# Modulation sums shared with GpSimd and a forget gate by quarters of the array, in a one-layer encoder kernel

## The chip, the cores and the metric

The kernel runs on one core of one Trainium2 chip. The metric is the device time of one execution in microseconds; the time before is the median of three executions. The core's engines are TensorE (PE in the profile), VectorE (DVE), ScalarE (ACT), GpSimd (POOL, called Pool here) and SyncE (SP), which only issues transfers here.

## What is computed

The reference is one layer of a hybrid encoder on 512 tokens of width 1024, all in f32. What matters here is its beginning:

```python
c_act = jax.nn.silu(c)
mod = c_act @ ada_w + ada_b                     # (1024) @ (1024, 6144)
sh1, sc1, g1, sh2, sc2, g2 = jnp.split(mod, 6, axis=-1)
h = modulate(rms_norm(x, mix_norm_g), sh1, sc1) # h * (1 + scale) + shift
z = h @ w_in                                    # q, k, v of mixers A and B, f_raw, ga, gb
log_f = jax.nn.log_sigmoid(f_raw + b_fgate)     # 8 heads: the forget gate
```

Behind it come two attention mixers (8 heads of 64 each), their merge, the output projection, and a mixture of 64 experts (top 8) with a shared expert. The change touches only the product c_act @ ada_w for sh1 and sc1, and the eight columns f_raw of h @ w_in.

## The kernel before, in words

**Modulation sums.** The 6144 columns of ada_w are taken in 24 steps of 256 columns, u = 0 to 23. A step's tile has 8 blocks k of 128 rows: [128, 8, 256]. ada_sum(u) on VectorE (lines 861 to 876) multiplies block 0 by the column cact[:, 0] (L871) and adds seven blocks, each times its own column of cact (L873), into one of four accumulators ACC (u mod 4). TensorE then sums over the 128 partitions with a matmul against ones. Steps 0 to 7 are sh1 and sc1, in pairs p = 0 to 3: ada_by_feature(u) (line 1300) brings the sum of step u into two PSUM columns, and mod_columns(p) on VectorE (line 895) makes of both steps the shift and scale columns for two blocks of h. Steps 8 to 23 are spread over all partitions, four at a time (spread_group, line 1350) and added to MOD. Their tiles go through two buffers AD; the tiles of the first eight steps have places of their own (AF, line 190).

**The head.** SyncE issues, in this order: the small rows, tiles 0 and 1, x in four parts, two blocks of w_in, tiles 2 and 3, two blocks of w_in, tiles 4 and 5, and so on to tile 7. VectorE does ada_sum(0) and ada_sum(1), then x_row(t) for the four token tiles (x times its reciprocal root; the roots come from ScalarE, L679 and L680) mixed with take_xt_first(t), the copy of half of the turned x out of PSUM; then three times two sums and mod_columns (lines 903 to 917). TensorE turns the rows, does ada_by_feature(0) and (1) between rows 1 and 2, and then project_first (line 1327): the first 512 columns of w_in with the contraction outermost, since block k of h can be used as soon as ScalarE has applied its shift and scale (modulate, line 690). Behind step k of it stands ada_by_feature(k + 2).

**The rest of the projection.** project(i, b) (line 1340) makes 512 further columns of z with h stationary, 32 matmuls of 128x128 by 512, on a block of w_in that SyncE loads into one of two places. Each f32 matmul has two records in the trace. forget (line 1318) makes the eight forget columns as 32 matmuls, h stationary [128x128], with 8 moving columns of WF. TensorE's order is written out: project_first, project(0, 1), forget, spread_group(0), project(1, 0), spread_group(1), project(1, 1), spread_group(2), the cumulative sum of log_f (L1368), project(2, 0) and so on (lines 1355 to 1376). VectorE's log_forget (line 919) follows sums 8 to 11; behind it come sums 12 to 23 and the additions mod_add (L879).

**SyncE's queue.** load_ada(u) (line 439) for u from 8 waits until sum u - 2 is done, since that frees its buffer. After load_ada(8) and load_ada(9) come load_w(1), the block for project(0, 1) (L446), then four rows of ada_b, the gain and the bias table (lines 466 to 476). Pool has nothing to do before the bias table lands (L559).

Of the kernel before, what the change touches and what calls it, by code (L numbers as in the profile page):

```python
# [25 lines left out]
P = 128  # L26
# [3 lines left out]
HA = 8  # L30
NH = 16
NT = S // P
KD = D // P
# [11 lines left out]
HC = 256  # L45
# [73 lines left out]
C_N = 1086 + NMAIN  # L119


def constants():

    c = np.zeros((P, C_N), np.float32)
    p = np.arange(P)[:, None]
    f = np.arange(P)[None, :]
    c[:, C_ID:C_ID + P] = p == f
    c[:, C_TEX:C_TEX + P] = p < f
    c[:, C_TIN:C_TIN + P] = p <= f
    c[:, C_ONE:C_ONE + P] = 1.0  # L130
    c[:, C_SLOT:C_SLOT + P] = f + 1
    token = p + P * np.arange(NT)[None]
    c[:, C_TOK2 + T_HI:C_TOK2 + 8:2] = token // 8 * 8 - NOTOK
    c[:, C_TOK2 + T_LO:C_TOK2 + 8:2] = token % 8
    c[:, C_M:C_M + NEXT] = np.arange(NEXT)[None]
    c[:, C_E:C_E + 1] = p
    c[:, C_LOW:C_LOW + 64] = (np.arange(8)[None, :] < np.arange(8)[:, None]).reshape(1, 64)
    c[:, C_SC:C_SC + 3] = [EPS, DH * EPS, 1.0]
    c[:, C_NEG1:C_NEG1 + P] = -1.0
    column = np.arange(E)  # L140
    c[:, C_CJ:C_CJ + NMAIN] = np.concatenate([column, SECOND])[None]
    cap = np.where(column < NFULL, P, P // 2)
    cap[SECOND[0]] = 2 * P
    cap[list(SECOND[1:])] = P + P // 2
    cap[NWIDE:NFULL] = NARROW
    c[:, C_CAP:C_CAP + E] = cap[None]
    c[:, C_LT:C_LT + E] = column[None] < p
    c[:, C_BR:C_BR + 2] = [3000.0, 2000.0]
    c[0:2, C_BC] = [3000.0, 2000.0]
    causal = np.zeros((P, S), np.float32)  # L150
    causal[:, S - P:] = np.where(f > p, NEG, 0.0)
    return c, causal


def build(nc, a):
# [4 lines left out]
    with st:  # L160
# [63 lines left out]
        def tab(at):  # L224
# [29 lines left out]
        WF = sb("WF", [P, KD, HA])  # L254
# [72 lines left out]
            "down_done", "o_ready", "row_index_ready"))  # L327
        s_out = sem("residual_written")
# [101 lines left out]
        def _(sp):  # L430
# [8 lines left out]
            def load_ada(u):  # L439
                sp.wait_ge(s_acc, u - 1)  # L440
                sp.dma_start(AD[:, u % 2], ada_step(u)).then_inc(s_ada[u % 2], 16)
# [24 lines left out]
            sp.dma_start(WF[:, :, :], w_in[:, 6 * SEG:6 * SEG + HA].rearrange(  # L466
# [18 lines left out]
            sp.wait_ge(s_acc, 24)  # L485
# [70 lines left out]
        def _(pool):  # L556
            pool.memset(CUM[:, :, :, 0:HA], 0.0).then_inc(s_pch, 1)
            pool.wait_ge(s_tab, 16)
# [3 lines left out]
            pool.wait_ge(s_acc, 24)  # L562
# [295 lines left out]
        def _(dve):  # L858
# [45 lines left out]
            ada_sum(1)  # L904
# [9 lines left out]
            for p in range(1, 4):  # L914
                ada_sum(2 * p)
                ada_sum(2 * p + 1)
                mod_columns(p)

            def log_forget():

                dve.wait_ge(s_f, 1)
                dve.wait_ge(s_small, 32)
                link(dve.tensor_tensor(FZ[:, 0], PS[:, 6, 0:32].rearrange("p (t h) -> p t h", t=NT),
# [350 lines left out]
        def _(pe):  # L1274
# [25 lines left out]
            def ada_by_feature(u):  # L1300

                p, r = u // 2, u % 2
                pe.wait_ge(s_acc, u + 1)
# [14 lines left out]
            def forget():  # L1318

                pe.wait_ge(s_wf, 16)  # L1320
                for t in range(NT):
                    for k in range(KD):
                        ins = mm(PS[:, 6, HA * t:HA * t + HA], HT[:, k, P * t:P * t + P], WF[:, k, :],
                                 start=k == 0, stop=k == KD - 1)
                ins.then_inc(s_f, 1)
# [24 lines left out]
            def spread_group(g):  # L1350
                pe.wait_ge(s_acc, 12 + 4 * g)
                need(pe, s_madd, 4 * g)
                spread(range(8 + 4 * g, 12 + 4 * g))
# [4 lines left out]
            spread_group(0)  # L1358
            project(1, 0)
# [5 lines left out]
            pe.wait_ge(s_cst, 16)  # L1365
# [358 lines left out]
```

## Time and profile before

| what | value |
|---|---|
| median of 3 executions | 1313.33 us (1310.59 to 1315.42) |
| the profiled execution, its own time | 1317.05 us |
| its span | 1315.1 us |
| mean granted TensorE clock | 0.964 |
| TensorE busy | 1211.5 us (92%), 4649 matmul records |
| VectorE, ScalarE, Pool busy | 480.9, 197.8, 192.7 us |

The profile is of one execution. Its times count from the start of the span. TensorE's matmuls overlap each other, so its busy time is not its useful time: what counts is when an instruction starts against the one before, and what ended the engine's idle time. The chain of waits, followed back from the last instruction, says which engine set the end at each moment.

### The profile page before, as it was taken

The numbers are of one execution on the slowest core, as the hardware profiler recorded it, in microseconds if no ns is written. First come the engines' busy times: TensorE is split into PE (matmuls) and PEld (weight loads), VectorE is DVE, ScalarE is ACT, GpSimd is POOL, SyncE is SP. The second block draws the span as 40 slices with busy tenths as digits, with TensorE's granted clock in tenths as the row PEclk, the third lists the DMA queues.
The fourth block names the chain that finished last, engine by engine and source line by source line (L and its number), as shares of the span: only waits on it lengthen the run. The fifth ranks groups of instructions, "written<-read, shape, count | busy, mean of one in ns | idle before, by whom it ended". The sixth has DMA issues, their size and how long they took to land.

```text
span 1315.1 us, 13938 instructions
## 1 busy us (share of the span) xinstructions
PE 1211.5 (92%) x4649; PEld 618.2 (47%) x4649; DVE 480.9 (37%) x1280; ACT 197.8 (15%) x451; POOL 192.7 (15%) x219
## 2 busy tenths in 40 slices
PE   4899999999999999998899999797999898999985
PEld 3455454444788644444444444343444343444442
DVE  5725457400466322455233233132233222333322
ACT  3211001110566101120011011010011001011100
POOL 0000000000221000000022222122222221313212
PEclk9998999999999999998899899899999899999988
DMA  9775562211100302165479999999989999989972
GB/s 323 248 268 192 192 220 107 81 64 64 65 0 0 128 1 104 64 256 240 189 281 361 395 359 360 374 358 374 373 287 378 388 367 388 381 268 376 360 207 34
DMA packets 87327, 311.51 MB, mean 237 GB/s; under 512 B 12225, under 2 KB 37985, under 8 KB 62049
## 3 DMA queue, kind: packets, MB, share of 16 engines
q1 hardware_dynamic: 71040, 272.77, 53.6%
q0 software_dynamic: 14784, 35.68, 11.6%
q10 hardware_dynamic: 1440, 2.27, 0.5%
q8 instruction: 35, 0.57, 0.2%
q14 instruction: 28, 0.22, 0.0%
HBM read 295.46 MB, written 34.08 MB: 251 GB/s over the span
## 4 chain that ended last, share of the span: by engine, by line
PE 74%; DMA 18%; DVE 3%; issue 2%; SPq 1%; ACT 1%; POOL 0%; DVEq 0%; POOLq 0%; ACTq 0%
PE PS L1634 19%; PE PS L1346 19%; PE PS L1655 9%; DMA R_WT<-w_up_e 9%; PE PS L1513 4%; PE PS L1484 4%; PE PS L1620 3%; PE PS L1417 2%; PE PS L1393 2%; DMA out<-second_sum 2%; DMA R_Z<-w_up_e 2%; DMA R_XM<-w_up_e 2%; PE PS L1523 2%; PE PS L1291 1%; PE PS L1405 1%
## 5 line engine op out<-in xcount | busy, mean ns | idle before, releaser
L1346 PE MATMUL PS<-R_WT,R_HT 128*128 128x512 f32 x576 | 248.9, 594 | 1.3 <-DMA R_WT<-w_in 1.3
L1634 PE MATMUL PS<-R_Z,R_G 128*128 128x512 f32 (+1 forms) x496 | 202.8, 627 | 12.8 <-DMA R_Z<-w_up_e 10.8
L1346 PEld LDWEIGHTS PS<-R_WT,R_HT 128*128 128x128 f32 x576 | 109.7, 191 | 138.2 <-issue 135.8
L1634 PE MATMUL PS<-R_WT,R_G 128*64 128x512 f32 (+1 forms) x400 | 144.2, 621 | 22.9 <-DMA R_Z<-w_up_e 18.0
L1209 DVE TENSOR_TENSOR R_G<-R_G,PS 128x256 f32<-128x256 f32 x50 | 30.5, 610 | 367.7 <-ACT R_G L821 367.7
L1634 PEld LDWEIGHTS PS<-R_Z,R_G 128*128 128x128 f32 (+1 forms) x496 | 75.6, 172 | 109.0 <-issue 109.0
L615 POOL DMA_INDIRECT R_G<-h_rows,gidx x54 | 56.1, 1040 | 447.7 <-DVE gidx L1198 371.5
L826 ACT ACTIVATE R_G<-PS 128x256 f32<-128x256 f32 x50 | 19.2, 385 | 572.8 <-PE PS L1642 556.8
L1655 PE MATMUL PS<-R_Z,R_G 128*128 128x512 f32 (+1 forms) x248 | 101.3, 610 | 0.8 <-issue 0.8
L1634 PEld LDWEIGHTS PS<-R_WT,R_G 128*64 128x64 f32 (+1 forms) x400 | 52.3, 160 | 100.7 <-issue 100.7
L1230 DVE SCALAR_TENSOR_TENSOR R_G<-PS,slx,R_XM 128x512 f32<-128x512 f32 x100 | 75.0, 751 | 63.5 <-PE PS L1655 63.5
L1634 PE MATMUL PS<-R_XM,R_G 128*128 128x512 f32 (+1 forms) x208 | 93.2, 601 | 4.4 <-DMA R_WT<-w_up_e 4.4
L621 POOL DMA_INDIRECT out<-R_G,ridx x38 | 55.9, 1470 | 106.9 <-DVE R_G L1230 48.8
L1655 PE MATMUL PS<-R_WT,R_G 128*64 128x512 f32 (+1 forms) x200 | 69.6, 599 | 0.0
L1620 PE MATMUL PS<-cst,R_G 128*128 128x128 f32 x416 | 56.7, 281 | 13.4 <-DMA R_G<-h_rows,gidx 12.5
L985 DVE CUSTOM_DVE_ANT_0 R_S<-PS,R_A 128x128 f32<-128x128 f32 (+1 forms) x64 | 28.9, 489 | 106.9 <-PE PS L1393 106.4
L873 DVE SCALAR_TENSOR_TENSOR R_A<-R_WT,cact,R_A 128x256 f32<-128x256 f32 x126 | 61.1, 485 | 4.5
L1620 PEld LDWEIGHTS PS<-cst,R_G 128*128 128x128 f32 x416 | 49.1, 146 | 14.8 <-DMA R_G<-h_rows,gidx 13.6
L1634 PEld LDWEIGHTS PS<-R_XM,R_G 128*128 128x128 f32 (+1 forms) x208 | 34.5, 168 | 45.6 <-issue 45.6
L1513 PE MATMUL PS<-R_Z,R_HT 128*128 128x512 f32 x128 | 55.4, 592 | 0.0
L1484 PE MATMUL PS<-R_WT 128*128 128x512 f32 x128 | 55.4, 592 | 0.0
L1655 PEld LDWEIGHTS PS<-R_Z,R_G 128*128 128x128 f32 (+1 forms) x248 | 35.6, 167 | 39.8 <-issue 39.7
(239 smaller groups left out, 1274.8 us busy)
## 6 DMA issues: line engine op xcount, KB each, us to landing
R_Z<-w_gate_e SPq DMA_DIRECT2D x26, 1024.0 KB, 12.6
R_Z<-w_up_e SPq DMA_DIRECT2D x26, 1024.0 KB, 22.9
R_Z<-w_down_e SPq DMA_DIRECT2D x26, 1024.0 KB, 18.2
R_WT<-w_gate_e SPq DMA_DIRECT2D x25, 1024.0 KB, 14.1
R_WT<-w_up_e SPq DMA_DIRECT2D x25, 1024.0 KB, 21.8
R_WT<-w_down_e SPq DMA_DIRECT2D x25, 1024.0 KB, 17.5
R_WT<-ada_w SPq DMA_DIRECT2D x18, 1024.0 KB, 6.8
R_WT<-w_in SPq DMA_DIRECT2D x9, 2048.0 KB, 10.2
```

Of the source, the lines that this page charges most:

```text
L615: pool.indirect_dma_start(out=XG[0:rows(j), b, :], out_offset=None, in_=h2_dram, in_offset=bass.IndirectOffsetOnAxis(ap=gidx[b][0:rows(j), ...
L621: pool.indirect_dma_start(out=sum_dram if n else a["out"], out_offset=bass.IndirectOffsetOnAxis(ap=index[0:part.shape[0], 0:1], axis=0), i ...
L873: ins = dve.scalar_tensor_tensor(acc, src[:, k], cact[:, k:k + 1], acc, ALU.mult, ALU.add)
L985: ins = dve.tensor_tensor_reduce(out=PB[:, b, at:at + w], in0=PS[:, g, src:src + w], in1=TB[:, b, S - w:S], scale=1.0, scalar=-3e38, op0=A ...
L1209: dve.tensor_tensor(AR[:, b, :].rearrange("p (k d) -> p d k", k=2), by_line(SIL[:, b, :], 2), by_line(PS[:, b, F:2 * F], 2), ALU.mult).the ...
L1230: dve.scalar_tensor_tensor(OB[:, b, 512 * half:512 * half + 512], PS[:, 2 + half, :], slx[:, bass.ds(j % 8, 1), 2:3].rearrange("p o c -> p ...
L1346: ins = mm(PS[:, t, :], HT[:, k, P * t:P * t + P], WR[:, b, k, :], start=k == 0, stop=k == KD - 1)
L1484: ins = mm(PS[:, 2 * half + r, :], YT[:, 4 * r + k, P * t:P * t + P], w[:, k, 512 * half:512 * half + 512], start=k == 0, stop=k == 3)
L1513: ins = mm(PS[:, n % 4, :], MT[:, k, P * t:P * t + P], WO[:, k, 512 * half:512 * half + 512], start=k == 0, stop=k == KD - 1)
L1620: ins = pe.transpose(PS[:, 4 + half, P * k:P * k + P], XG[:, b, 512 * half + P * k:512 * half + P * k + P], ident)
L1634: ins = mm(PS[w * h:w * h + w, b, :].rearrange("p (g n) -> p g n", g=2), XT[:, b, k, w * h:w * h + w], WGU[n][:, k], start=k == 0, stop=k ...
L1655: ins = mm(PS[w * h:w * h + w, 2 + half, :], AT[:, b, k, w * h:w * h + w], WDN[n][:, k, 512 * half:512 * half + 512], start=k == 0, stop=k ...
```

## The change

Part one: the forget gate. WF is padded from 8 to 32 columns of zeros and lies in a free part of R_G; Pool sets it to zero first and SyncE's load of it waits for that. forget makes eight matmuls with WF stationary, [128x32], and h moving, 512 columns; block k goes to the columns 32 (k mod 4) to 32 (k mod 4) + 31 of the array, so that four partial results stand in the four quarters of bank 6. VectorE copies the bank to FT, and forget_rows turns and adds the four quarters with FT stationary and a constant of eight columns that has ones in rows h, 32 + h, 64 + h and 96 + h. It stands behind spread_group(0) on TensorE.

Part two: Pool does the sums of steps 1, 3, 5 and 7, in four instructions each: the whole tile times cact, spread over the 256 columns, in place, and additions of the upper half of the blocks to the lower, of 1024, 512 and 256 elements per partition. VectorE keeps steps 0, 2, 4, 6 and all from 8. The counts that the others wait for change with it: s_accp counts Pool's sums, and SyncE's load of step 9 waits for all four of them.

```diff
--- before.py
+++ after.py
@@ -116,7 +116,8 @@
 C_TEX, C_TIN, C_SLOT = 264, 392, 520
 C_TOK2, C_M, C_E, C_LOW, C_NEG1 = 648, 656, 700, 701, 765
 C_CJ, C_CAP, C_LT, C_BR, C_BC = 893, 893 + NMAIN, 957 + NMAIN, 1021 + NMAIN, 1085 + NMAIN
-C_N = 1086 + NMAIN
+C_SEL = 1086 + NMAIN
+C_N = C_SEL + HA
 
 
 def constants():
@@ -147,6 +148,8 @@
     c[:, C_LT:C_LT + E] = column[None] < p
     c[:, C_BR:C_BR + 2] = [3000.0, 2000.0]
     c[0:2, C_BC] = [3000.0, 2000.0]
+    for h in range(HA):
+        c[h::32, C_SEL + h] = 1.0
     causal = np.zeros((P, S), np.float32)
     causal[:, S - P:] = np.where(f > p, NEG, 0.0)
     return c, causal
@@ -251,7 +254,8 @@
         rbias = sb("rbias", [P, E])
         TABS = R_G[:, 1024:1024 + HA * NTAB].rearrange("p (h n) -> p h n", h=HA)
         EXTS = R_G[:, 4096:4096 + HA * EXT].rearrange("p (h n) -> p h n", h=HA)
-        WF = sb("WF", [P, KD, HA])
+        WF = R_G[:, 7168:7168 + 32 * KD].rearrange("p (k h) -> p k h", k=KD)
+        FT = R_S[:, 3072:3584]
         FZ = sb("FZ", [P, 4, NT, HA])
         CUM = sb("CUM", [P, 2, NT, NH])
         mx = sb("mx", [P, 2, 2, NT])
@@ -325,6 +329,8 @@
             "onehot_ready", "slots_done", "slot_rows_ready", "x_transposed", "xt_ready_dve",
             "xt_ready_act", "gu_done", "silu_ready", "act_ready", "act_transposed", "at_ready",
             "down_done", "o_ready", "row_index_ready"))
+        s_accp, s_plink = sem("ada_sums_ready_pool"), sem("pool_sum_chain")
+        s_wfz, s_ft = sem("wf_padding_set"), sem("forget_parts_taken")
         s_out = sem("residual_written")
         s_sout = [sem(f"shared_written{b}") for b in range(2)]
         s_etab = sem("main_experts_ready")
@@ -437,7 +443,10 @@
                 return ada_w[:, ADA_COLS[u]:ADA_COLS[u] + HC].rearrange("(k p) n -> p k n", p=P)
 
             def load_ada(u):
-                sp.wait_ge(s_acc, u - 1)
+                if u == 9:
+                    sp.wait_ge(s_accp, 4)
+                else:
+                    sp.wait_ge(s_acc, max(4, u - 5))
                 sp.dma_start(AD[:, u % 2], ada_step(u)).then_inc(s_ada[u % 2], 16)
 
             def load_w(c):
@@ -463,7 +472,8 @@
                 first_ada(2 * q + 1)
                 first_w(q)
             sp.dma_start(cst[:, C_FIRST:C_N], a["consts"][:, C_FIRST:C_N]).then_inc(s_cst, 16)
-            sp.dma_start(WF[:, :, :], w_in[:, 6 * SEG:6 * SEG + HA].rearrange(
+            sp.wait_ge(s_wfz, 1)
+            sp.dma_start(WF[:, :, 0:HA], w_in[:, 6 * SEG:6 * SEG + HA].rearrange(
                 "(k p) n -> p k n", p=P)).then_inc(s_wf, 16)
             load_ada(8)
             load_ada(9)
@@ -482,7 +492,7 @@
 
             sp.wait_ge(s_ext, 3)
             sp.dma_start(ext_dram, EXTS).then_inc(s_extw, 16)
-            sp.wait_ge(s_acc, 24)
+            sp.wait_ge(s_acc, 20)
             sp.wait_ge(s_extw, 16)
             sp.dma_start(T4[:, 0:HA, S - 2 * P:S], bass.AP(
                 ext_dram.tensor, P - 1, [[HA * EXT - 1, P], [EXT, HA], [1, 2 * P]])).then_inc(s_t4, 16)
@@ -554,12 +564,24 @@
 
         @block.gpsimd
         def _(pool):
+            pool.memset(WF[:, :, :], 0.0).then_inc(s_wfz, 1)
             pool.memset(CUM[:, :, :, 0:HA], 0.0).then_inc(s_pch, 1)
+            link = Chain(pool, s_plink)
+            pool.wait_ge(s_cact, 2)
+            for u in range(1, 8, 2):
+                acc = ACC[:, u % 4]
+                pool.wait_ge(s_af[u], 16)
+                need(pool, s_ada1, u - 3)
+                src = AF[u]
+                link(pool.tensor_tensor(src, src, bc(cact[:, :].unsqueeze(2), [P, KD, HC]), ALU.mult))
+                link(pool.tensor_tensor(src[:, 0:4], src[:, 0:4], src[:, 4:8], ALU.add))
+                link(pool.tensor_tensor(src[:, 0:2], src[:, 0:2], src[:, 2:4], ALU.add))
+                pool.tensor_tensor(acc, src[:, 0], src[:, 1], ALU.add).then_inc(s_accp, 1)
             pool.wait_ge(s_tab, 16)
             pool.tensor_copy(EXTS[:, :, P - 1:EXT - 1], TABS[:, :, NTAB - 1:0:-1]).then_inc(s_ext, 1)
             pool.tensor_copy(EXTS[:, :, 0:P - 1], bc(TABS[:, :, NTAB - 1:NTAB], [P, HA, P - 1])).then_inc(s_ext, 1)
             pool.tensor_copy(EXTS[:, :, EXT - 1:EXT], TABS[:, :, 0:1]).then_inc(s_ext, 1)
-            pool.wait_ge(s_acc, 24)
+            pool.wait_ge(s_acc, 20)
             pool.tensor_copy(T4[:, 0:HA, 0:S - 2 * P], bc(TABS[:, :, NTAB - 1:NTAB], [P, HA, S - 2 * P]))\
                 .then_inc(s_t4f, 1)
             pool.wait_ge(s_t4, 16)
@@ -901,7 +923,6 @@
                     .then_inc(s_mcol, 1)
 
             ada_sum(0)
-            ada_sum(1)
             x_row(0)
             x_row(1)
             take_xt_first(0)
@@ -913,14 +934,15 @@
             take_xt_first(3)
             for p in range(1, 4):
                 ada_sum(2 * p)
-                ada_sum(2 * p + 1)
                 mod_columns(p)
 
             def log_forget():
 
                 dve.wait_ge(s_f, 1)
+                dve.tensor_copy(FT, PS[:, 6, :]).then_inc(s_ft, 1)
+                dve.wait_ge(s_f, 2)
                 dve.wait_ge(s_small, 32)
-                link(dve.tensor_tensor(FZ[:, 0], PS[:, 6, 0:32].rearrange("p (t h) -> p t h", t=NT),
+                link(dve.tensor_tensor(FZ[:, 0], PS[:, 7, 0:32].rearrange("p (t h) -> p t h", t=NT),
                                        bc(bfg[:, :].unsqueeze(1), [P, NT, HA]), ALU.add))
                 link(dve.tensor_scalar(FZ[:, 1], FZ[:, 0], -1.0, None, ALU.mult))
                 dve.tensor_tensor(FZ[:, 1], FZ[:, 0], FZ[:, 1], ALU.min).then_inc(s_e, 1)
@@ -1300,7 +1322,7 @@
             def ada_by_feature(u):
 
                 p, r = u // 2, u % 2
-                pe.wait_ge(s_acc, u + 1)
+                pe.wait_ge(s_accp if r else s_acc, p + 1)
                 need(pe, s_mcol, p - 1)
                 for half in range(2):
                     n = 2 * r + half
@@ -1318,10 +1340,17 @@
             def forget():
 
                 pe.wait_ge(s_wf, 16)
+                for k in range(KD):
+                    g = k % 4
+                    ins = mm(PS[32 * g:32 * g + 32, 6, :], WF[:, k, :], HT[:, k, :], start=k < 4, stop=k >= 4)
+                ins.then_inc(s_f, 1)
+
+            def forget_rows():
+
+                pe.wait_ge(s_ft, 1)
                 for t in range(NT):
-                    for k in range(KD):
-                        ins = mm(PS[:, 6, HA * t:HA * t + HA], HT[:, k, P * t:P * t + P], WF[:, k, :],
-                                 start=k == 0, stop=k == KD - 1)
+                    ins = mm(PS[:, 7, HA * t:HA * t + HA], FT[:, P * t:P * t + P], cst[:, C_SEL:C_SEL + HA],
+                             start=True, stop=True)
                 ins.then_inc(s_f, 1)
 
             def project_first():
@@ -1348,7 +1377,7 @@
                     ins.then_inc(s_proj, 1)
 
             def spread_group(g):
-                pe.wait_ge(s_acc, 12 + 4 * g)
+                pe.wait_ge(s_acc, 8 + 4 * g)
                 need(pe, s_madd, 4 * g)
                 spread(range(8 + 4 * g, 12 + 4 * g))
 
@@ -1356,13 +1385,14 @@
             project(0, 1)
             forget()
             spread_group(0)
+            pe.wait_ge(s_cst, 16)
+            forget_rows()
             project(1, 0)
             spread_group(1)
             project(1, 1)
             spread_group(2)
 
             pe.wait_ge(s_lf, 1)
-            pe.wait_ge(s_cst, 16)
             for t in range(NT):
                 for j in range(t + 1):
                     ins = mm(PS[:, 7, HA * t:HA * t + HA], cst[:, C_TIN:C_TIN + P] if j == t else ones,
```

## Rows read from the trace of the kernel before

**Rows 1.** The page, part 4: the chain that ended last, share by engine
```profile
PE 74%; DMA 18%; DVE 3%; issue 2%; SPq 1%; ACT 1%; POOL 0%; DVEq 0%; POOLq 0%; ACTq 0%
```

**Rows 2.** The chain in order of time, 0 to 330 us: start, us, what
```profile
53.49 10.38 DMA R_WT<-w_in
...
63.92 27.73 PE PS L1346 x64
91.65 11.18 PE PS L1323 x64
102.83 3.61 PE PS L1280 x8
106.45 28.14 PE PS L1346 x64
134.59 1.73 PE PS L1280 x8
136.32 27.47 PE PS L1346 x64
...
165.51 2.13 PE PS L1368 x20
```

**Rows 3.** Busy time by stretch: start:end, length, busy (count) by engine, PEclk, DMA share, GB/s
```profile
97.00:103.00 6.00, 6.00 (x29) 6.00 (x29) 0.13 (x1) 0.00 (x0) 0.00 (x0) 0.50 0.00 0
```

**Rows 4.** Timeline of TensorE, expert stage, halves: start, us, engine, line, operation
```profile
721.81 0.59 PE L1655 MATMUL PS<-R_Z,R_G 128*64 128x512 f32 x1
...
722.24 0.59 PE L1655 MATMUL PS<-R_Z,R_G 128*64 128x512 f32 x1
722.25 0.59 PE L1655 MATMUL PS<-R_XM,R_G 128*64 128x512 f32 x1
```

**Rows 5.** Timeline of VectorE: a bank's copy, the forget bias, additions behind sum 15
```profile
18.82 0.69 DVE L892 COPY R_HT<-PS 128x512 f32<-128x512 f32 x1 [1.20 <-PE PS L1291]
...
102.87 0.19 DVE L923 TENSOR_TENSOR FZ<-PS,bfg 128x32 f32<-128x32 f32 x1 [19.01 <-PE PS L1323]
...
123.61 1.41 DVE L879 TENSOR_TENSOR R_XM<-R_XM,PS 128x256 f32<-128x256 f32 x4
```

**Rows 6.** Timeline of the head: VectorE's sums, ScalarE's first root, the columns of two pairs
```profile
7.99 0.35 DVE L871 TENSOR_SCALAR R_A<-R_Z,cact 128x256 f32<-128x256 f32 x1 [7.99 <-DMA R_Z<-ada_w]
8.38 3.61 DVE L873 SCALAR_TENSOR_TENSOR R_A<-R_Z,cact,R_A 128x256 f32<-128x256 f32 x7
...
13.41 0.29 ACT L680 ACTIVATE ssx<-ssx,cst 128x1 f32<-128x1 f32 x1
...
15.81 0.16 DVE L885 RECIPROCAL ssx<-ssx 128x1 f32<-128x1 f32 x1
...
35.59 0.16 DVE L898 TENSOR_TENSOR mcol<-PS,gcol 128x4 f32<-128x4 f32 x1 [1.16 <-PE PS L1307]
...
44.87 0.16 DVE L898 TENSOR_TENSOR mcol<-PS,gcol 128x4 f32<-128x4 f32 x1 [0.99 <-PE PS L1307]
```

**Rows 7.** DMA issues of tiles 1, 3 and 7: count, KB, us from issue to landing
```profile
R_Z<-ada_w SPq DMA_DIRECT2D x1, 1024.0 KB, 8.0
...
R_Z<-ada_w SPq DMA_DIRECT2D x1, 1024.0 KB, 15.8
...
R_WT<-ada_w SPq DMA_DIRECT2D x1, 1024.0 KB, 17.0
```

**Rows 8.** Groups by line and shape, Pool: xcount, busy us, mean ns, idle before
```profile
L559 POOL COPY R_G<-R_G 128x2048 f32<-128x2048 f32 x1 | 1.9, 1894 | 72.1 <-DMA R_G<-rel_bias 72.1
...
L600 POOL CAST R_HT<-cst 128x904 bf16<-128x904 f32 x1 | 1.5, 1457 | 141.4 <-PE PS L1513 141.4
```

**Rows 9.** Timeline 555 to 560 us, and line 1056: ns min/median/max, first and last start
```profile
556.66 0.69 DVE L1055 TENSOR_TENSOR R_G<-PS,R_XM 128x512 f32<-128x512 f32 x1 [5.45 <-PE PS L1513]
556.69 1.46 POOL L600 CAST R_HT<-cst 128x904 bf16<-128x904 f32 x1 [141.40 <-PE PS L1513]
...
L1056 DVE TENSOR_TENSOR R_XM<-R_XM,R_G x8: 691/693/1199, 507.6 to 557.4; 128x512 f32<-128x512 f32 x8
```

## The prediction

> **What bounds the kernel now.** I read the chain of waits first, for the engine that sets the end: TensorE holds 74% of it and DMA 18% [rows 1]. The chain in order of time shows where the change sits. Up to 53.5 us it runs through VectorE's modulation sums, the turning of x and project_first; at 53.49 SyncE issues the load of the second block of w_in and the chain is that transfer until 63.88. From 63.92 to beyond 300 us it is TensorE without a gap: project, the forget gate for 11.18 us, a spread of 3.61 us, project for 28.14, a spread of 1.73, project for 27.47 [rows 2]. So a microsecond taken off TensorE behind 63.9 us shows whole, and one before it shows as far as that w_in load and TensorE's own arrival both come earlier. The later stages start from TensorE's counts (the expert weights are first loaded when the output projection is done), so they shift along.
>
> The stretch table adds the clock [rows 3]: from 97 to 103 us it is 0.50, the lower of TensorE's levels (1.2 against 2.4 GHz), while the engine does the forget gate's 64 records of 8 columns. The next steps still pay for it: the first spread takes 3.61 us and a later one 1.73, project(1, 0) takes 0.67 more than the project behind it [rows 2]. A later short run of such small matmuls goes at 0.11 us a record (20 in 2.13 us [rows 2]) where these take 0.17, so being small alone does not lower the clock.
>
> **Part one: the forget gate.** Removed: 11.18 us, the spread's surplus of 1.88 and project's 0.67 [rows 2]. Added: eight matmuls of 512 columns, each two records as everywhere here, every fourth on the same 32 columns of the array. No row shows quarters. The nearest are halves: a pair starts 0.01 us apart and the pairs follow each other every 0.43 us [rows 4], so the halves overlap whole. If quarters do so too, 16 records take 4 times 0.43, 1.7 us; if only two overlap, 3.4; if none, 6.9. I take 1.7 with 0.2 for the change of shape: 1.9. Then four selections of 8 columns, 8 records at 2.13/20 = 0.11 us: 0.9. Between them VectorE copies the bank, 0.69 us [rows 5], under the spread's 1.73; its queue is free there, since it sat idle 19.0 us before the forget bias [rows 5]. What stands behind that copy now: log_forget starts after forget_rows; it is a chain of five small VectorE and two ScalarE instructions, some 3 us, that ran beside the long spread until now, so sum 12 begins some 3 us later against TensorE. Sum 15 and its additions are through at 125.0, the next spread is at 134.6 [rows 2, 5]: cover of 9.6 us, so nothing. The memset of the padded weights, the wait for it and eight more columns of constants cost nothing: the load of WF is issued at 36 us and used at 91. The work of the path is 1.9 + 1.7 + 0.9 = 4.5 in place of 11.2 + 3.6 + 0.7 = 15.5: **minus 11.0 us**, between minus 11.2 and minus 5.8 (no overlap).
>
> **Part two: Pool's sums.** VectorE's sum is eight instructions; the seven additions take 3.61 us, and two sums go from 7.99 to 15.8, 3.9 us each [rows 6]. Without it x_row(0) could start when ScalarE has the first root, 13.7, and not at 15.81: 2.1 us [rows 6]. Behind that the loop goes by TensorE's two steps of project_first and their columns: from one pair's columns to the next it takes 9.28 us (35.59 to 44.87 [rows 6]), of which VectorE's two sums fill 7.8. Taking sums away from VectorE shortens no lap. So there is little to win: about 2 us at the head, and w_in's load bounds even that, because it is now queued behind Pool's last sum (SyncE waits for it before the load of step 9; behind that wait stand w_in's second block, four bias rows, the gain and the bias table, the last of which Pool itself needs only at 73 us). The tiles for Pool land at 10.9 (issued at 2.9, 8.0 us under way), 23.4 (7.6 and 15.8) and, the last, 42.2 (25.2 and 17.0) [rows 7].
>
> The price of Pool's sum: no row has a two-input operation on Pool. A one-input copy of 2048 elements takes 1.894 us, 0.92 ns an element; a cast of 904 takes 1.457, 1.61 ns [rows 8]. The sum has 2048 + 1024 + 512 + 256 = 3840 elements. Lower end, the copy's rate: 3.6 us. Upper end, twice the cast's rate: 12.4. Two operands at the copy's rate give 1.85 ns; for the arithmetic and four starts I go some way towards the upper end and take 2.3: 4.7 + 2.4 + 1.2 + 0.6 = **8.8 us**. The Trainium skill (GPSIMD Engine Reference, section 3.1) gives 4497 ns for such an addition over 2048 elements; by it the sum would be 8.4 us as an estimate. Alone, four such sums just keep up: the last starts when its tile lands at 42.2 and ends at 51.
>
> They are not alone. One place shows Pool and VectorE together on SBUF. Pool's cast runs from 556.69 to 558.15; VectorE's L1055, with one input in PSUM, runs through it in its 0.69 us; L1056, with both inputs in SBUF, starts at 557.4 and takes 1.199 where the median of its eight is 0.693 [rows 9]. It lost 0.51 us of the 0.77 that the cast still had. Were the two sharing evenly it would lose at most half of the overlap, 0.38. So I read it as VectorE held until Pool's reading is over. The Trainium skill (SBUF — State Buffer, section "Who interferes with whom") says it as a rule: a VectorE instruction with two SBUF inputs and a Pool instruction that reads SBUF exclude each other, the first holding for its whole length; the trace agrees. Every instruction of VectorE's sums has the tile and the accumulator as inputs. If what the stretched L1056 shows holds for them, the two serialise:
> - Head: Pool's first multiplication starts at 10.9 and holds 4.7 us; VectorE's last instructions of sum 0 go between Pool's four, so sum 0 ends near 19 (12 now) and row 0 is ready some 4 us later than now. Pool's second sum starts at 23.4, between rows 1 and 2, and its multiplication holds these for 3 more: project_first starts 7 us later.
> - Laps: 8.8 + 3.9 = 12.7 us and the small instructions in place of 9.28, three times: 3.6 each, 11 us.
>
> Together **plus 18**. Ends: if the copy's rate held, Pool would be done in time and it would be about 0; if Pool's instructions come in the worst order (the small column update stuck behind a multiplication) and the clock drops in the gaps, as it did when the forget gate left the array thinly used [rows 3], plus 26; if VectorE wins each turn, the head loses 3 and the last lap has no Pool sum left, plus 10.
>
> **Sum.** 18 - 11 = plus 7. The profiled execution took 1317.05 for a span of 1315.1, 3.7 above the median of 1313.33; it is against its rows that plus 7 stands, and I carry it over to the median: **1320 us**.
>
> **Rivals.**
> - No exclusion (other side): one stretched instruction is thin evidence, and the sums could slide past each other. Then the head is 1.5 to 2 earlier, Pool's last sum ends at 51, the w_in load goes at 51.5, and 10.4 us later [rows 2] TensorE has it, 2 us before now. 1313.3 - 11 - 2 = 1300. It decides at the first multiplication: if VectorE's additions beside it still follow each other every 0.52 us (3.61 for seven), this is the case. For it: L1055 beside the same cast lost nothing; against: L1055 has one input in SBUF, and the sums have two. Chance 0.34.
> - Even sharing: where both work VectorE's sum stretches to 8 us; beside Pool's 8.8 to 10 the laps are 9.5 to 10, nothing is gained at the head: 3 - 11, 1305. Chance 0.10.
> - Exclusion, the forecast: 1313.3 - 11 + 10 to + 26, 1312 to 1328; chance 0.52, half of it over 1320.
> - Quarters don't overlap (the change doesn't do what it says): minus 5.8 and not 11 for part one: 1325 beside the exclusion, 1305 without it. Chance 0.04 beside the others.
>
> **How the numbers follow.** About 0.5%, 6.6 us, can be told from no change. Faster by more: no exclusion 0.34, most of even sharing 0.07, a rest: 0.42. Within: the milder half of exclusion and remnants: 0.29. Slower: 0.29. The likeliest case's own range is 1312 to 1328; the range over the cases, 1299 to 1327, leaves out the tails.
>
> **What would show it.** In the changed profile: sixteen records of the forget gate in 1.7 us from first to last start; clock 1.00 through the stretch after it, the spread at 1.73 us; four Pool multiplications of 4.7 us at some 10.9, 23 to 24, and then later; VectorE's L873 group (the additions into the sum) with a longest far over its median, ending with Pool's instruction; laps of the columns at 12.9 us or more; project(0, 1) starting at 80 rather than 64. I am wrong if L873 keeps its pace beside Pool, and the laps at 9.3: then the time is near 1300. A Pool multiplication of under 2.5 us would bring the same.

## The result, and the profile after

The changed kernel takes 1324.98 us (median of 5, 1320.91 to 1325.73) against 1313.33 before (1310.59 to 1315.84): a ratio of 1.0083, 95% interval 1.0061 to 1.0106. The profiled execution took 1324.98 us for a span of 1323.2; the span before was 1315.1. The same kernel was run a second time (further down), with nearly the same ratio.

The chain's shares, in the page of the changed kernel, answer to [rows 1]:

```profile
PE 70%; DMA 20%; DVE 5%; issue 2%; SPq 2%; ACT 0%; POOL 0%; DVEq 0%; POOLq 0%; ACTq 0%
```

VectorE has gone from 3% to 5% and DMA from 18% to 20%; Pool holds 0%. That alone is a warning: the engine that received the work is not on the chain, and the one that was relieved is. The chain in order of time (start, us, what) answers to [rows 2]:

```profile
68.52 12.80 DMA R_WT<-w_in
...
81.37 27.73 PE PS L1375 x64
109.10 1.85 PE PS L1345 x16
110.96 1.92 PE PS L1302 x8
112.88 0.79 PE PS L1352 x8
113.67 27.57 PE PS L1375 x64
```

Two things are to be read here, of opposite sign. project(0, 1) starts at 81.37, where it was 63.92: the head has lost 17.45 us. And from there to the start of project(1, 0) it takes 32.30 us and not 42.53, with 0.57 less in project(1, 0) itself: the forget gate has won 10.80. The difference is 6.65 us, and the two traces stand 6.65 apart when the chain enters its last uninterrupted run of project (203.59 against 196.94).

The wait in front of project(0, 1) is booked on the load of w_in, but the load was late because its queue was. SyncE issues it at 68.52, behind the tiles of steps 8 and 9, and these went out at 67.49, when VectorE had done its last sum of the head (Pool's had been done since 56.2). Once issued, the load took 12.80 us for 10.38. It cost little: TensorE came to the end of project_first only at 80.92 (62.60 before) and waited 0.45 us for the block, where it had waited 1.32.

Where the head lost its time is in Pool's and VectorE's timelines (start, us, engine, line, operation, idle before). Pool:

```profile
10.74 3.60 POOL L576 TENSOR_TENSOR R_Z<-R_Z,cact 128x2048 f32<-128x2048 f32 x1 [9.61 <-DMA R_Z<-ada_w]
14.42 2.41 POOL L577 TENSOR_TENSOR R_Z<-R_Z 128x1024 f32<-128x1024 f32 x1
...
23.17 3.60 POOL L576 TENSOR_TENSOR R_Z<-R_Z,cact 128x2048 f32<-128x2048 f32 x1 [3.80 <-DMA R_Z<-ada_w]
...
47.88 3.60 POOL L576 TENSOR_TENSOR R_WT<-R_WT,cact 128x2048 f32<-128x2048 f32 x1 [7.71 <-PE PS L1329]
```

VectorE:

```profile
8.09 9.02 DVE L895 SCALAR_TENSOR_TENSOR R_A<-R_Z,cact,R_A 128x256 f32<-128x256 f32 x7
...
23.21 4.11 DVE L910 TENSOR_SCALAR R_S<-R_XM,ssx 128x1024 f32<-128x1024 f32 x1
...
31.07 10.43 DVE L895 SCALAR_TENSOR_TENSOR R_A<-R_Z,cact,R_A 128x256 f32<-128x256 f32 x7
47.77 0.16 DVE L920 TENSOR_TENSOR mcol<-PS,gcol 128x4 f32<-128x4 f32 x1 [6.28 <-PE PS L1329]
47.97 3.53 DVE L922 SCALAR_TENSOR_TENSOR mcol<-mcol,gcol 128x2 f32<-128x2 f32 x1
...
63.18 0.16 DVE L920 TENSOR_TENSOR mcol<-PS,gcol 128x4 f32<-128x4 f32 x1 [4.58 <-PE PS L1329]
...
72.46 0.16 DVE L920 TENSOR_TENSOR mcol<-PS,gcol 128x4 f32<-128x4 f32 x1 [5.00 <-PE PS L1329]
```

Seven additions that took 3.61 us [rows 6] take 9.02 and 10.43. The row of x at 23.21, 0.75 us where nothing holds it, takes 4.11 and ends at 27.32; Pool's multiplication ran from 23.17 to 26.77. Most telling is the update of two columns, L922: 128x2 elements, 3.53 us, from 47.97 to 51.50, beside Pool's multiplication from 47.88 to 51.48. VectorE is booked as busy in all of this. In a table of busy times it looks like work; only the longest of a group whose median is unchanged shows that it is waiting:

```profile
L895 DVE SCALAR_TENSOR_TENSOR R_A<-R_WT,cact,R_A x119: 483/485/486, 63.8 to 189.0; 128x256 f32<-128x256 f32 x119
L895 DVE SCALAR_TENSOR_TENSOR R_A<-R_Z,cact,R_A x21: 483/485/3926, 8.1 to 58.1; 128x256 f32<-128x256 f32 x21
```

(line 895: ns min/median/max, first and last start). From 63.8 on, when Pool has done its last sum, nothing exceeds 486 ns.

### The profile page after: what moved, and what is told of

The parts are those of the page before. It is cut to its first block, busy times and chain, and to the rows that moved or that the text cites. A ratio compares the mean times of both kernels' runs of the same rounds, so it can differ in the third digit from the quotient of the medians.

```text
span 1323.2 us, 13847 instructions
## 1 busy us (share of the span) xinstructions
PE 1203.3 (91%) x4609; PEld 604.2 (46%) x4609; DVE 491.7 (37%) x1249; ACT 197.4 (15%) x451; POOL 226.2 (17%) x236
## 4 chain that ended last, share of the span: by engine, by line
PE 70%; DMA 20%; DVE 5%; issue 2%; SPq 2%; ACT 0%; POOL 0%; DVEq 0%; POOLq 0%; ACTq 0%
PE PS L1375 19%; PE PS L1664 18%; DMA R_WT<-w_up_e 9%; PE PS L1685 9%; PE PS L1543 4%; PE PS L1514 4%; DMA R_XM<-w_up_e 3%; PE PS L1447 2%; PE PS L1650 2%; DVE R_A L895 2%; PE PS L1423 2%; DMA out<-second_sum 2%; DMA R_Z<-w_up_e 2%; PE PS L1553 2%; DMA R_G<-h_rows,gidx 1%
## 5 line engine op out<-in xcount | busy, mean ns | idle before, releaser
L1664 PE MATMUL PS<-R_Z,R_G 128*128 128x512 f32 (+1 forms) x496 | 199.7, 617 | 12.1 <-DMA R_Z<-w_up_e 8.3
L1664 PE MATMUL PS<-R_WT,R_G 128*64 128x512 f32 (+1 forms) x400 | 146.9, 640 | 21.0 <-DMA R_Z<-w_up_e 12.8
L1664 PE MATMUL PS<-R_XM,R_G 128*128 128x512 f32 (+1 forms) x208 | 96.0, 616 | 8.6 <-DMA R_WT<-w_up_e 8.6
L1685 PE MATMUL PS<-R_Z,R_G 128*128 128x512 f32 (+1 forms) x248 | 100.5, 606 | 0.8 <-issue 0.8
L1685 PE MATMUL PS<-R_WT,R_G 128*64 128x512 f32 (+1 forms) x200 | 69.6, 599 | 0.0
L895 DVE SCALAR_TENSOR_TENSOR R_A<-R_WT,cact,R_A 128x256 f32<-128x256 f32 x119 | 57.7, 485 | 4.3
```

Of the source, the lines that this page charges most:

```text
L895: ins = dve.scalar_tensor_tensor(acc, src[:, k], cact[:, k:k + 1], acc, ALU.mult, ALU.add)
L1664: ins = mm(PS[w * h:w * h + w, b, :].rearrange("p (g n) -> p g n", g=2), XT[:, b, k, w * h:w * h + w], WGU[n][:, k], start=k == 0, stop=k ...
L1685: ins = mm(PS[w * h:w * h + w, 2 + half, :], AT[:, b, k, w * h:w * h + w], WDN[n][:, k, 512 * half:512 * half + 512], start=k == 0, stop=k ...
```

## The experiments

Each kernel was timed beside the kernel before on the same chip. The kernel before took 1314.56 us (17 runs) beside the gate alone (first time), Pool's sums alone and VectorE's sums in PSUM; 1312.89 (23 runs) beside "Pool only writes", "One quarter for all" and "The old forget matmuls"; and 1313.82 (13 runs) beside the other four. Differences "by the medians" are against that value.

### The forget gate alone

The changed kernel without Pool's loop, and the counts as before (the cut is shortened):

```diff
-            for u in range(1, 8, 2):
...
-                pool.tensor_tensor(acc, src[:, 0], src[:, 1], ALU.add).then_inc(s_accp, 1)
...
             ada_sum(0)
+            ada_sum(1)
...
                 ada_sum(2 * p)
+                ada_sum(2 * p + 1)
```

> The forget gate by quarters alone, all sums on VectorE. The two parts are independent on the path, in my account: the head is as before (project(0, 1) starts at 63.9), then 1.85 + 1.92 + 0.79 us, as in the changed kernel's chain, in place of 11.18 + 3.61, and 0.57 less in project(1, 0). Expected 10.8 us under the kernel before, 1302 to 1303. Rival: the later stages take the gain back (waits on expert weights); then under 6 us. Second rival, that the gain needs Pool's freed VectorE time: the copy of bank 6 would come late and the selections start over 0.3 us behind the spread.

Measured: 1305.46 us, ratio 0.9919 (0.9888 to 0.9949). The chain:

```profile
64.21 27.73 PE PS L1363 x64
91.95 1.85 PE PS L1333 x16
93.80 1.93 PE PS L1290 x8
95.72 0.79 PE PS L1340 x8
96.52 27.57 PE PS L1363 x64
```

The head is as before (project(0, 1) starts 0.3 us later) and the gate as in the changed kernel, so the part works alone. VectorE's copy of the bank starts at 93.87 and the selections stand right behind the spread, so it doesn't lean on a relieved VectorE. Behind the projection the chain is 10.5 us earlier (186.43 against 196.94). By the medians the gain is smaller than the 10.8 expected: 9.1 us here, and 7.4 in a second set of runs (1306.42 us, ratio 0.9947, 0.9927 to 0.9967), whose interval, 4 to 10 us, leaves 10.8 out. No run shows where the rest of the gain is lost.

### Pool's sums alone

The changed kernel with the old forget matmuls; WF, its load and the forget bias are as in the kernel before too (not shown):

```diff
-                for k in range(KD):
-                    g = k % 4
-                    ins = mm(PS[32 * g:32 * g + 32, 6, :], WF[:, k, :], HT[:, k, :], start=k < 4, stop=k >= 4)
+                for t in range(NT):
+                    for k in range(KD):
+                        ins = mm(PS[:, 6, HA * t:HA * t + HA], HT[:, k, P * t:P * t + P], WF[:, k, :],
+                                 start=k == 0, stop=k == KD - 1)
```

> Pool's sums alone, the forget gate as before. If the loss in the head is Pool's and additive, project(0, 1) starts at 81.4 as in the changed kernel, and the time is 17.5 us over the kernel before on the span (1331) or, by the medians (plus 11.65 and the 10.8 of the gate), up to 22 over (1336). Rival: the loss comes from the gate's own preparations (the memset of WF, SyncE's wait for it); then the head is as before, 63.9, and the time within 3 us of the kernel before.

Measured: 1333.49 us, ratio 1.0129 (1.0090 to 1.0169), 18.9 us over by the medians.

```profile
83.22 27.73 PE PS L1363 x64
110.95 10.07 PE PS L1340 x64
121.03 3.61 PE PS L1297 x8
124.64 27.60 PE PS L1363 x64
```

project(0, 1) starts at 83.22, 1.9 us later than expected, and the loss is there without the new gate. The gate's old price is back with it, less 1.1 us (10.07 for 11.18): the granted clock stayed at 1.00 to about 114.5, 3.5 us into the 64 records, where before it had fallen by 94, 2.4 us into them. The rival, that the preparations of WF cost the head, falls, since the head loses without them here and loses nothing with them in the gate alone.

### VectorE's sums in PSUM

The same work on both engines; only the place of VectorE's running sum differs.

```diff
+                part = PS[:, 5 - (u // 2) % 2, HC:2 * HC] if u < 8 else acc
-                    ins = dve.scalar_tensor_tensor(acc, src[:, k], cact[:, k:k + 1], acc, ALU.mult, ALU.add)
+                    ins = dve.scalar_tensor_tensor(acc if k == KD - 1 else part, src[:, k], cact[:, k:k + 1], part,
+                                                   ALU.mult, ALU.add)
```

> The changed kernel with VectorE's running sum of steps 0, 2, 4, 6 in PSUM, so that its additions have one input in SBUF; Pool works as before it. If two inputs in SBUF beside a reading Pool are what holds VectorE, the additions (L895's place) keep a pace of some 0.52 to 0.58 us through Pool's multiplications, the laps fall from 19.9, 15.4 and 9.3 us to 9.3 to 11 (the small update of the columns still has two SBUF inputs and may wait up to 3.6), project(0, 1) starts at 62 to 66 and the time is 1301 to 1307. Rival, that Pool blocks VectorE whatever its inputs, or that the semaphores of Pool's chain do: the additions still stretch to 3.9 us, and the time stays at 1320 or more. Rival, that Pool itself is too slow for the laps: additions unstretched but laps over 12 us with TensorE waiting for Pool's count.

Measured: 1308.59 us, ratio 0.9954 (0.9933 to 0.9975), some 16 us under the changed kernel for the place of the running sum. Line 896 (ns min/median/max) and, in the timeline of VectorE, what was still held:

```profile
L896 DVE SCALAR_TENSOR_TENSOR PS<-R_Z,cact,PS x18: 490/490/491, 9.0 to 43.3; 128x256 f32<-128x256 f32 x18
```

```profile
15.79 2.62 DVE L912 TENSOR_SCALAR R_S<-R_XM,ssx 128x1024 f32<-128x1024 f32 x1
...
25.00 2.54 DVE L924 SCALAR_TENSOR_TENSOR mcol<-mcol,gcol 128x2 f32<-128x2 f32 x1
```

and the last addition of a sum, which writes to SBUF, beside Pool:

```profile
42.03 3.60 POOL L576 TENSOR_TENSOR R_WT<-R_WT,cact 128x2048 f32<-128x2048 f32 x1 [1.79 <-DMA R_WT<-ada_w]
43.83 0.48 DVE L896 SCALAR_TENSOR_TENSOR R_A<-R_Z,cact,PS 128x256 f32<-128x256 f32 x1
```

Eighteen additions took 490 to 491 ns, more than half of them beside one of Pool's instructions (3.60 us a multiplication, as before): neither Pool's being active nor its semaphores hold VectorE, nor is Pool too slow. The edit moves the place that the additions write to as well; but the last addition of each sum reads PSUM and writes SBUF, and it takes 0.48 us beside Pool's multiplication, so it is the input that counts. The size was missed: project(0, 1) starts at 67.57, not by 66, and the laps (from one pair's columns to the next) were 14.6, 9.8 and 9.3 us, the first well over the 11 expected. The two kinds of instruction above are still held, and the first step of project_first took 5.92 us for 3.67. In the changed kernel that step took 5.83 us with a granted clock of 0.50 for most of it (26 to 35.5 us), but the rows of this trace give 1.00 there, so the cause stays open.

### The update of the columns too

```diff
-                dve.scalar_tensor_tensor(mcol[:, 1, k], mcol[:, 1, k], 1.0, gcol[:, 0, k], ALU.add, ALU.mult)\
+                dve.scalar_tensor_tensor(mcol[:, 1, k], mcol[:, 1, k], 1.0, PS[:, 5, KD + 2 * p:KD + 2 * p + 2], ALU.add, ALU.mult)\
```

> The changed kernel with VectorE's sums in PSUM and the update of the columns (L924, held up to 2.54 us there) reading its gain from PSUM too, so with one input in SBUF. What is left to be held are only the rows of x. If the exclusion is what holds the update, it takes 0.16 us in all four places, project_first starts some 2 us earlier than with the sums alone in PSUM, project(0, 1) at 64 to 66 in place of 67.6. Rival: the update waits for something else (its gain, TensorE); then it is as long as before.

Measured: 1304.31 us, ratio 0.9921 (0.9896 to 0.9946).

```profile
24.61 0.16 DVE L924 SCALAR_TENSOR_TENSOR mcol<-mcol,PS 128x2 f32<-128x2 f32 x1
...
35.58 0.16 DVE L924 SCALAR_TENSOR_TENSOR mcol<-mcol,PS 128x2 f32<-128x2 f32 x1
...
44.85 0.16 DVE L924 SCALAR_TENSOR_TENSOR mcol<-mcol,PS 128x2 f32<-128x2 f32 x1
```

All four take 0.16 us (the first stands inside a multiplication of Pool, 23.54 to 27.14), and project(0, 1) starts at 64.42, 0.5 us later than in [rows 2]: with no second SBUF input in VectorE's sums and updates, Pool's sums cost next to nothing. They win nothing either. One row of x is still held (2.62 us), so project_first starts at 27.45, where the gate alone has it at 27.42 to 27.44. And the load of w_in leaves 3.3 us earlier than before but takes 14.22 us for 10.38, so TensorE waits for it for 2.04. The median is 1304.31 beside 1306.42 of the gate alone in the same set, with intervals that overlap.

### Pool only writes

```diff
-                link(pool.tensor_tensor(src, src, bc(cact[:, :].unsqueeze(2), [P, KD, HC]), ALU.mult))
+                link(pool.memset(src, 0.0))
...
-                pool.tensor_tensor(acc, src[:, 0], src[:, 1], ALU.add).then_inc(s_accp, 1)
+                pool.memset(acc, 0.0).then_inc(s_accp, 1)
```

> The changed kernel with Pool's four instructions of a sum replaced by memsets of the same tiles (2048, 1024, 512, 256 elements): Pool only writes. It leaves out the scale of the first modulation (steps 1, 3, 5, 7 are zero), so the routing and the later stages differ and only the head is read. If it is Pool's reading that excludes VectorE's second SBUF input, VectorE's additions all stay at 0.485 us beside the memsets (some 1.9 us for the first, by 0.96 for 1024 in the trace), laps 9.3 us. If any use of SBUF by Pool holds VectorE, one addition beside each first memset takes up to 1.9 us more.

There is one execution (1304.21 us), and only its head is read. A memset from 10.89 to 12.69 takes the place of the first multiplication. Lines 895 and 893 (ns min/median/max), and the memset beside the longest of line 893:

```profile
L895 DVE SCALAR_TENSOR_TENSOR R_A<-R_Z,cact,R_A x21: 483/485/486, 8.3 to 41.9; 128x256 f32<-128x256 f32 x21
...
L893 DVE TENSOR_SCALAR R_A<-R_Z,cact x3: 352/354/740, 7.9 to 38.4; 128x256 f32<-128x256 f32 x3
...
26.15 0.74 DVE L893 TENSOR_SCALAR R_A<-R_Z,cact 128x256 f32<-128x256 f32 x1
...
26.22 0.53 POOL L578 MEMSET R_Z<- 128x512 f32 x1
```

The additions, two SBUF inputs and all, are untouched beside the memsets: it is Pool's reading that holds them. But the TENSOR_SCALAR from SBUF to SBUF was held: 0.74 us at 26.15, beside a memset that ran from 26.22 to 26.75. That I had not expected. The second and third laps were 9.3 us, as expected (updates at 38.3, 47.6 and 56.9); the first was 13.9, 10.96 before, with a first step of project_first of 6.61 us for 3.67, again at a granted clock of 1.00 in the rows.

### One quarter for all

```diff
-                    g = k % 4
+                    g = 0
```

with start at the first and stop at the last of the eight, and a selection constant for the one quarter alone, on top of the gate alone.

> The forget gate alone as in the first experiment, but all eight matmuls on the first 32 columns of the array. If the gain of quarters is that four run at once, the 16 records now take 16 x 0.43 = 6.9 us from first to last start in place of 1.85, and the time is 5 us over that of the first experiment. Rival: a stationary of 32 columns is cheap by itself (the records follow each other faster than 0.43 us); then the two are within 1 us.

Measured: 1310.03 us, ratio 0.9974 (0.9955 to 0.9993), 4.6 us over the gate alone by the medians (of two sets). The chain:

```profile
91.37 6.98 PE PS L1333 x16
```

6.98 in place of 1.85: matmuls on different quarters do run four at a time, and a narrow stationary is not cheap in itself.

### The old forget matmuls, between the tiles

The kernel before; forget(t) behind each token tile of project(0, 1).

```diff
-            project(0, 1)
-            forget()
+            project(0, 1, forget)    # calls forget(t) behind tile t
```

> The kernel before with its forget matmuls (unchanged, 8 moving columns) moved into project(0, 1), a quarter of them behind each token tile. If half of their cost was the clock that fell, each group of 16 records takes 16 x 0.107 = 1.7 us, the clock stays at 1.00, the spread behind takes 1.73 and project(1, 0) 27.5: the gate costs 6.9 us and not 11.2 + 1.9 + 0.6, the time is 6 to 7 us under the kernel before (1306 to 1307). Rival: 0.175 us a record is what such a matmul costs whatever the clock; then 11.2 us stay and at most 2.5 are won.

Measured: 1308.61 us, ratio 0.9975 (0.9958 to 0.9991), 4.3 us under the kernel before by the medians.

```profile
69.16 1.68 PE PS L1322 x16
...
95.12 1.68 PE PS L1322 x16
96.80 1.83 PE PS L1280 x8
98.63 27.47 PE PS L1346 x64
```

Unchanged instructions, 0.105 us a record: the gate costs 6.7 us, the spread 1.83 and project(1, 0) 27.47. Against 11.18, 3.61 and 28.14 that is 6.9 us of path, and the granted clock is 1.00 from 69 to 107 us. So about half of what the old forget gate cost (11.18 and the 2.5 behind it) was the clock it brought down. By the medians less shows than the 6 to 7 us expected (interval 1 to 6 us), as with the gate by quarters. This trace also had a head 2 us shorter than the others, because the second half of the turning of x took 1.07 and 1.10 us for eight records where the kernel before takes 1.9; the granted clock is 1.00 in the rows of both, so the reason stays open.

### The changed kernel again

> The changed kernel unedited, once more. In the trace it was 6.65 us late when the projection had settled (203.6 against 196.9), and 11.65 by the medians. If the 5 us between are of the expert stage's own scatter (680 to 687 us from its first matmul to the end over the kernels run so far, in no order with the change), this run gives 5 to 9 us over the kernel before. If the changed kernel makes the expert stage longer, it gives 10 to 14 again and its stage takes 684 us or more.

Measured: 1324.58 us, ratio 1.0084 (1.0063 to 1.0105), so 10.8 by the medians: in time the case of a longer expert stage. But its expert stage, from the first expert matmul to the end, took 679.8 us where the first profile had 684.7 and the kernel before 680.1. So neither side of the expectation holds as put: the difference is repeated, and this stage is short. The profiled execution was the fastest of the six, though (1320.69 us), so its trace can't say where the median's excess lies. A part of the difference lies in the profiled execution of the kernel before:

```profile
430.00:440.00 10.00, 8.76 (x69) 7.89 (x68) 4.78 (x11) 3.42 (x11) 0.00 (x0) 0.94 0.01 2
440.00:450.00 10.00, 10.00 (x31) 5.70 (x30) 0.69 (x1) 2.30 (x4) 0.00 (x0) 0.89 0.64 242
```

(stretches of the kernel before; the column behind the engines is the clock). At the end of its attention the clock dips, and from the first turn_qk to the output projection it takes 165.7 us (334.1 to 499.8) where the changed kernel takes 163.9 (340.8 to 504.7). Seven of the other traces have 163.9 or 164.0 there, and the kernel with the columns in PSUM 165.6, so it is an episode of an execution and not of the change. That is 1.8 of the 3.7 us by which the profiled execution stood over its median.

### Without Pool: the first sum cut up

On top of the gate alone. VectorE does sum 1 in pieces between the rows of x; w_in's block is loaded ahead of the tiles of steps 8 and 9. The cut is shortened.

```diff
+            load_w(1)
             load_ada(8)
             load_ada(9)
-            load_w(1)
...
             ada_sum(0)
-            ada_sum(1)
+            sum_one((0, 1, 2))
             x_row(0)
+            sum_one((3, 4))
             x_row(1)
+            sum_one((5,))
             take_xt_first(0)
             x_row(2)
+            sum_one((6, 7))
             take_xt_first(1)
...
             ada_by_feature(0)
-            ada_by_feature(1)
             turn_row(2)
+            ada_by_feature(1)
             turn_row(3)
```

> The forget gate by quarters alone, with what Pool's sums were to bring reached without Pool: sum 1 on VectorE cut into pieces between the rows of x, which otherwise waited for it, TensorE's second column step one row later, and w_in's second block issued ahead of steps 8 and 9 (its place is free from the start). Row 0 is ready near 14.6 in place of 16.8, project_first starts near 25.3 in place of 27.5, project(0, 1) follows it without waiting for a load, near 61 in place of 64: 2 to 3 us under the forget gate alone, 1300 to 1303. Rival: the turning of x is bounded by TensorE and ScalarE, not by VectorE's sum; then project_first starts within 0.5 us of where it did.

and for the gate alone beside it:

> The forget gate by quarters alone, unedited, once more beside the next: 9 to 12 us under the kernel before.

The gate alone, 1306.42 us, was 7.4 us under the kernel before and not 9 to 12. The kernel with the sum cut up took 1303.22 us, ratio 0.9917 (0.9898 to 0.9936), 3.2 us under the gate alone in the same set. The chain:

```profile
54.76 7.10 PE PS L1368 x16
61.86 27.47 PE PS L1380 x64
```

project(0, 1) follows project_first with no load between, at 61.86 (63.63 in the gate alone). Row 0 was ready at 14.7, as expected, but project_first began at 26.93 and not at 25.3, only 0.5 us before the 27.42 of the gate alone: that is the rival's case. The cut-up sum brought next to nothing, and 1.3 of the trace's 1.8 us come from the earlier load. The turning of x took 1.9 us for each eight records, as it does at a granted clock of 0.50 in the changed kernel (1.97 at 27.38), though the rows give 1.00 here. By the medians it is 10.6 us under the kernel before and 21 under the changed kernel.

## Why the prediction was right

The forecast was 1320, by exclusion of the two engines in the head; measured were 1325, by that mechanism. That the time lies in the stated range says less: 1299 to 1327 covers both signs, and the chances put "faster" (0.42) over "slower" (0.29). What stood the test is the mechanism, which had 0.52.

- **The forget gate**, minus 11.0: minus 10.80 on the path. The quarters took 1.85 (1.9), the selections 0.79 (0.9), the spread 1.92 (1.7); the clock was 1.00 from 109 to 114 us. One quarter for all took 6.98, the 6.9 that the sum gave as its upper end. Sum 12 started 3 us later against TensorE and cost nothing.
- **Exclusion**, read from the one stretched L1056 [rows 9]: shown by three edits. Without Pool's reading (memsets) the additions stay at 0.485, without VectorE's second SBUF input (in PSUM) at 0.490, and the same change on the column update takes it from 2.54 to 0.16. The length held goes by Pool's instruction: additions and updates of 3.5 to 3.9 us beside a multiplication of 3.6. The Trainium skill (SBUF — State Buffer, section "Who interferes with whom") had the rule; the trace agrees with it.
- **The head**, plus 18: plus 17.45. That the total came so close is luck, for its parts did not. Row 0 was ready at 18.8 (forecast some 4 us later than 16.8: it was 2), and project_first started 3.5 us later, not 7: Pool's second sum came beside the last row of x and not between rows 1 and 2. Behind that TensorE lost 14.8 us to the end of project_first, not 11, and it then waited 0.9 us less for w_in. The laps were 19.9, 15.4 and 9.3 us where I had 12.9 three times (before: 10.96, 9.28 and 9.28). Pool went ahead with sum 5 while VectorE was still in sum 2, so the first lap carried the exclusion by the end of sum 3 and by sum 5, the second that by sum 7, and the last had none. At the start of the first two the updates were held (1.53 and 3.53 us), as in the worst order named, and TensorE's step in the first lap ran partly at a granted clock of 0.50 behind its wait, which cost 1.7 us of the path. And the load of w_in was not behind Pool's last sum, as the forecast had it, but behind VectorE's. TensorE:

```profile
41.55 0.61 PE L1329 MATMUL PS<-cst,R_A 128*128 128x1 f32 x4 [4.51 <-DVE R_A L895]
42.02 5.38 PE L1363 MATMUL PS<-R_WT,R_HT 128*128 128x512 f32 x8
```

(timeline in the changed kernel; from 59.13 on such a step takes 3.68 us).
- **The price of Pool's sum**, 8.8 us: the four instructions of the first took 8.40 (8.63 from 10.74 to 19.37), those of the others 8.1 to 8.3. The multiplication took 3.60, not 4.7; the additions of 1024, 512 and 256 took 2.35, 1.26 and 0.73 where nothing held them (in the two kernels with the sums in PSUM), close to the 2.4, 1.2 and 0.6 assumed. The 4497 ns of the Trainium skill (GPSIMD Engine Reference, section 3.1) are for an addition of 2048 elements; here the multiplication, with one operand spread from eight values, took less, and the measurement decides.
- **What was mis-sized** is the last step: "it is against its rows that plus 7 stands, and I carry it over to the median". The traces do stand 6.65 us apart behind the projection, 4.9 behind the attention (there the kernel before had lost 1.8 by the clock), 3.5 at the first expert matmul and 8.1 at the end. The medians stand 11.65 and 10.8 apart, with intervals from 8.0 and 8.3 up. The profiled execution of the kernel before stood 3.7 us over its median, and the one of the changed kernel at its median: those 3.7 us are what the carrying over lost, and 1.8 of them are shown, as an episode of that execution. The parts run alone say the same by their medians: Pool's sums plus 18.9, the gate minus 9.1 and minus 7.4, together 9.8 to 11.5. So against 17.45 and 10.80 on the path some 1.5 us more were lost and 1.7 to 3.4 less won, and where these lie stays open. The expert stage scatters by more than that over the traces (679.7 to 686.8 us, leaving out the kernel that only writes), but I have not shown that it is this.
- **The no-exclusion rival** would have been 1300. The kernel in which exclusion is edited away takes 1304.31, 9.5 us under the kernel before of its set where the rival had 13: the 2 us at the head did not come (project(0, 1) at 64.42, not 62), and by the medians the gate wins less than 11.

## What to carry to other kernels

Before moving work from VectorE to Pool, list what VectorE does beside it: instructions with two SBUF inputs waited for the end of the reading Pool instruction, however small they were (3.53 us for an update of 0.16), and a chain of eight short ones against four long ones turned a shared job into a queue. If the overlap is wanted, give VectorE's second operand a place in PSUM; here that took the loss away and still won nothing. And price small matmuls by the clock they leave behind: cut up between large ones, the same 64 records cost 6.7 us and not 11.2, and next to nothing after them. Last, the best kernel here (1303.22 us) got most of what its trace shows over the gate alone from issuing one load earlier.

## What the runs showed of the hardware

- A VectorE TENSOR_SCALAR from SBUF to SBUF was held by Pool though it has one tensor input: a row of x took 4.11 us for 0.75 beside a multiplication, and one of 256 elements 0.74 for 0.35 beside a memset, which only writes. It is fast where it is free (0.75 us for 1024 elements, where the additions take 0.485 for 256). With its output in PSUM the one of 256 elements took 0.47 to 0.49 us and was not held beside Pool's addition (28.07 in "VectorE's sums in PSUM"). Copies out of PSUM (0.68 and 0.69 us) were never held.
- Pool's multiplication by an operand spread from eight values takes 3.60 us for 2048 elements, 1.76 ns an element; its addition of two full operands of 1024 takes 2.35 us, 2.3 ns an element. Whether the operation or the spread operand makes it cheaper was not tested.
- The granted clock in the rows does not explain every slow stretch of TensorE: in the head, eight records of the turning of x took 1.9 us in some traces and 1.07 in others, all at 1.00 in the rows.
- VectorE's additions with the running sum in PSUM take 0.490 us, with it in SBUF 0.485.
